# Three placements in on-chip memory moved by 16, 32 and 64 bytes

## The reference

```python
for l in range(2):
    hc, hx = ada_ffn_half(hc, ...), ada_ffn_half(hx, ...)      # first SwiGLU
    uc, ux = modulate(rms_norm(hc)), modulate(rms_norm(hx))
    yc, yx = token_mixing(uc, ux, ...)                         # three branches
    hx = hx + gate * yx
    hx = ada_ffn_half(hx, ...)                                 # second SwiGLU
    if l == 0: hc = hc + gate * yc; hc = ada_ffn_half(hc, ...)

ada_ffn_half = h + 0.5 * gate * ((silu(g) * u) @ w_down),  g, u = split(mod(rms_norm(h)) @ w_gu)
token_mixing: p = u @ w_in;  gMLP branch | bidirectional gated DeltaNet | latent attention;
              y = (sum_b sigmoid(gate_b) * (branch_b @ w_b)) @ w_out
```

## The kernel before

| tensor | start before | start after | step from one part to the next, before | after |
|---|---|---|---|---|
| w_hi | 25728 | 25728 | 4096 a half | 4128 |
| w_lo | 38016 | 38112 | 4096 a half | 4128 |
| h | 50304 | 50560 | 2048 a chunk | 2048 |
| u_hi | 66688 | 66944 | 2048 a chunk | 2064 |
| u_lo | 83072 | 83456 | 2048 a chunk | 2064 |
| arena | 127808 | 128384 | 2048 a slot | 2048 |

## Time and profile before

### The profile page before, as it was taken

The page is one execution under the profiler, slowest core; times in us unless marked ns, Lnnn a source line. Parts: engine busy times, 40 slices in busy tenths (PEclk is TensorE's granted clock), DMA queues, the critical chain, the costliest instruction groups (busy, mean ns, idle before and its releaser), DMA issues.

```text
span 2531.9 us, 37811 instructions
## 1 busy us (share of the span) xinstructions
PE 2430.3 (96%) x15806; PEld 2061.2 (81%) x15806; DVE 1466.0 (58%) x2287; ACT 945.7 (37%) x1537; POOL 90.4 (4%) x122
## 2 busy tenths in 40 slices
PE   5999999999989999999999999999999989999999
PEld 4888877867878888888888788888886878898999
DVE  5877656355667465577655453333354667567555
ACT  2322223365554422232222232322245554444543
POOL 0000000000023000000000000000000003100000
PEclk9999999999999999999999999999999999999999
DMA  7544543201200143335454332222321220055454
GB/s 274 215 181 185 183 150 114 87 34 51 84 35 2 34 166 124 126 117 200 183 199 166 150 110 100 100 96 98 107 100 67 84 84 2 19 177 173 167 184 167
DMA packets 44663, 309.65 MB, mean 122 GB/s; under 512 B 5072, under 2 KB 6224, under 8 KB 7632
## 3 DMA queue, kind: packets, MB, share of 16 engines
q1 hardware_dynamic: 44208, 305.98, 33.5%
q10 hardware_dynamic: 288, 1.27, 0.1%
HBM read 306.18 MB, written 1.05 MB: 121 GB/s over the span
## 4 chain that ended last, share of the span: by engine, by line
PE 89%; DVE 5%; ACT 3%; issue 2%; DMA 1%; SPq 0%; POOL 0%; ACTq 0%; DVEq 0%
PE bank L1475 74%; PE bank L1841 7%; PE bank L1468 2%; PE bank L1778 1%; PE bank L1757 1%; DVE w_lo L2097 1%; DVE u_lo L2144 1%; DVE sq L2136 1%; PE bank L1506 1%; ACT w_hi L933 1%; PE bank L1691 1%; DMA mod_par<-in_mod 0%; PE bank L1518 0%; PE bank L1766 0%; ACT work L1246 0%
## 5 line engine op out<-in xcount | busy, mean ns | idle before, releaser
L2097 DVE TENSOR_TENSOR w_lo<-ring,w_hi 128x1024 fp32r<-128x1024 f32 x420 | 510.5, 1224 | 676.5 <-ACT w_hi L933 671.7
L1475 PE MATMUL bank<-u_hi,w_hi 128*128 128x512 f32 (+1 forms) x2272 | 816.7, 359 | 27.9 <-DVE w_lo L2097 14.9
L1475 PE MATMUL bank<-u_hi,w_lo 128*128 128x512 f32 (+1 forms) x2272 | 805.8, 355 | 0.0
L1475 PE MATMUL bank<-u_lo,w_hi 128*128 128x512 f32 (+1 forms) x2272 | 805.3, 354 | 0.0
L933 ACT ACTIVATE w_hi<-ring 128x1024 fp32r<-128x1024 f32 x420 | 442.9, 1059 | 837.7 <-PE bank L1475 824.1
L1475 PEld LDWEIGHTS bank<-u_hi,w_hi 128*128 128x128 f32 x2272 | 432.9, 191 | 95.6 <-issue 21.6
L1475 PEld LDWEIGHTS bank<-u_lo,w_hi 128*128 128x128 f32 x2272 | 433.0, 191 | 59.4
L1475 PEld LDWEIGHTS bank<-u_hi,w_lo 128*128 128x128 f32 x2272 | 433.3, 191 | 56.8
L1475 PE MATMUL bank<-hidden_hi,w_hi 128*128 128x512 f32 (+1 forms) x722 | 260.6, 361 | 0.0
L1475 PE MATMUL bank<-hidden_lo,w_hi 128*128 128x512 f32 (+1 forms) x722 | 259.9, 360 | 0.0
L1475 PE MATMUL bank<-hidden_hi,w_lo 128*128 128x512 f32 (+1 forms) x722 | 259.9, 360 | 0.0
(11 more groups left out here) (236 smaller groups left out, 2458.1 us busy)
## 6 DMA issues: line engine op xcount, KB each, us to landing
ring<-in_wts SPq DMA_DIRECT2D x288, 1024.0 KB, 4.8
h<-in_x SPq DMA_DIRECT2D x8, 256.0 KB, 4.1
par<-in_par ACTq DMA_DIRECT2D x2, 620.0 KB, 6.0
out<-h SPq DMA_DIRECT2D x8, 128.0 KB, 4.2
cst<-in_cst SPq DMA_DIRECT2D x1, 704.0 KB, 11.8
mod_par<-in_mod SPq DMA_DIRECT2D x1, 96.0 KB, 12.0
cond<-in_c SPq DMA_DIRECT2D x1, 8.0 KB, 1.8
```

The costliest lines, as they stand in the source:

```text
L1475: last = weights.used(pe.matmul(out, lhs[a], rhs[b], start=start and n == 0, stop=stop and n == 2))
L2097: tt(w_lo[:, b % HALVES, :], half_source(n % RING, part), w_hi[:, b % HALVES, :].bitcast(F32), ALU.subtract).then_inc(panel_left[n % RING] ...
```

## The change

Nothing is computed differently and no instruction is added, removed or moved: on all five queues the built program has the same instructions in the same order with the same waits. Only addresses change. Each half of w_hi and w_lo gets 8 unused elements (32 bytes) behind it, each chunk of u_hi and u_lo 4 unused elements (16 bytes). 64 unused bytes stand behind the weights and 64 ahead of the arena. The table above has the addresses that come of it.

```diff
+W_GAP = 8
+U_GAP = 4
...
-        w_hi = sb("w_hi", [P, HALVES, HALF], F32R)
-        w_lo = sb("w_lo", [P, HALVES, HALF], F32R)
-
-        products_kept = [nc.alloc_sbuf_tensor_at(f"products_kept{n}", [P, 2 * HALVES, T], F32,
-                                                 offset=weights_at + n * HALVES * HALF * 4) for n in range(2)]
+        w_hi = sb("w_hi", [P, HALVES, HALF + W_GAP], F32R)
+        w_lo = sb("w_lo", [P, HALVES, HALF + W_GAP], F32R)
+
+        products_kept = [nc.alloc_sbuf_tensor_at(f"products_kept{n}", [P, HALVES, HALF + W_GAP], F32,
+                                                 offset=weights_at + n * HALVES * (HALF + W_GAP) * 4) for n in range(2)]
+        sb("behind_weights", [P, 16])
         h = sb("h", [P, DC, T])
-        u_hi = sb("u_hi", [P, DC, T], F32R)
-        u_lo = sb("u_lo", [P, DC, T], F32R)
+        u_hi = sb("u_hi", [P, DC, T + U_GAP], F32R)
+        u_lo = sb("u_lo", [P, DC, T + U_GAP], F32R)
...
         SLOT = T * 4
+        sb("ahead_of_arena", [P, 16])
         base = -(-nc.sbuf_base // 32) * 32
...
-            return [x[:, 2 * b:2 * b + 2, :] for x in products_kept]
+            return [x[:, b, 0:HALF].rearrange("p (d t) -> p d t", t=T) for x in products_kept]
...
-                act.activation(w_hi[:, b % HALVES, :], half_source(n % RING, part), ACT.Copy).then_inc(weights_rounded, 1)
+                act.activation(w_hi[:, b % HALVES, 0:HALF], half_source(n % RING, part), ACT.Copy).then_inc(weights_rounded, 1)
...
-                    return [x[:, b % HALVES, :].rearrange("p (k n) -> p k n", n=width) for x in (w_hi, w_lo)]
+                    return [x[:, b % HALVES, 0:HALF].rearrange("p (k n) -> p k n", n=width) for x in (w_hi, w_lo)]
...
-                tt(w_lo[:, b % HALVES, :], half_source(n % RING, part),
-                   w_hi[:, b % HALVES, :].bitcast(F32), ALU.subtract).then_inc(
+                tt(w_lo[:, b % HALVES, 0:HALF], half_source(n % RING, part),
+                   w_hi[:, b % HALVES, 0:HALF].bitcast(F32), ALU.subtract).then_inc(
```

## The result

The changed kernel takes 2552.93 us (2548.54 at a mean granted clock of 0.988 and 2557.31 at 0.982) against 2534.88 us: a ratio of 1.0069, with a 95% interval from 1.0047 to 1.0092. It is 18 us slower. That lies within the 2% that I called no change and inside my range, but the forecast was 47 us the other way.

The account below looks back on a forecast made before the run. The prediction took the pace of TensorE's fp32r products as the bound. Its terms, -17.4 and -29.9 us for u and 0 for the rest, sum to -47.3 us: 2488 us forecast, range 2435 to 2555.

Parts of the forecast that it names:

- What bounds the kernel: Claimed the pace of TensorE's fp32r products sets the time, 74% of the last-ending chain, with the producers ahead.
- Term 1: Gaps between u's chunks and weight halves: u one step faster, -17.4 us at 256 columns and -29.9 at 512.
- the two steps of the sum: The forecast's -17.4 us for u at 256 columns and -29.9 us for u at 512.
- its own sign of failure: Forecast fails if the sum's first two steps differ in sign, or VectorE's waits before the products grow over 10 us.
- Term 2: Arena 64 bytes later: 0 taken, with 21 us up or 47.5 us down as its range.
- Terms 3 and 4: VectorE and ScalarE at new addresses, and producers or weight transfers becoming late: 0 taken, no gain taken back.
- No net effect: Rival on TensorE's paces: distances are not the cause or their spread only averages, +4 us; 2505 to 2550 us, chance 0.28.
- the case that had a chance of 0.12: The slower outcome, a time above 2550 us.
- Most of the excess goes: Rival: both new spreads avoid a coincidence, saving 68.4 to 142 us on TensorE; 2393 to 2470 us, chance 0.24.
- Slower, by a 64-byte unit: Rival: operand starts off 64 bytes cost one step more, +35.5 us, 2570 us, or 2601 with weights; chance 0.12.
- The page's rule: TensorE's two SBUF reads use independent ports and never wait, so the sum would be 0: 2535 us.

Follow-up runs that it names:

- e1_map: Separate kernel without the backbone: TensorE alone runs groups of 24 fp32r matmuls at many operand distances; 226.6 to 234.6 ns at 512 columns, 113.3 to 120.0 at 256.
- e9_map3: Separate kernel, TensorE's groups of 24 matmuls at 16 distances, six each, after pauses of different length; distance 0 always came to 226.7 ns at 512 columns.
- e2_swap: Kernel before with u and arena exchanging their places modulo 512, weights unmoved, no gaps; 2550.55 us, ratio 1.0063.
- e7_arena: Kernel before with only the 64 bytes ahead of the arena; 2529.88 us against 2534.21, ratio 0.9979.
- e6_starts: Kernel before with w_lo, u and arena starting where the changed kernel has them modulo 512, but no gaps between chunks or halves; 2559.31 us, ratio 1.0099.
- e3_chunks: Kernel before with only the 16 bytes behind each chunk of u, other starts kept modulo 512; 2552.91 us, ratio 1.0071.
- e5_map2: Separate kernel without the backbone, varying weight width, starts by 4 bytes, chunk step and columns; 512-column groups with full-width weights settled between 226.7 and 240.0 ns.
- e11_late: Kernel before with the arena 64 bytes later, and u and hidden of layer 1's last SwiGLU 192 bytes into their chunks; 2526.28 us against 2535.07, ratio 0.9959.
- e8_best: Kernel before with starts moved so that every distance is -16 modulo 256; 2548.55 us, ratio 1.0056.
- e10_halves256: Kernel before with 256-byte gaps between weight halves and the arena 64 bytes later, every distance 0 modulo 256; 2524.81 us, ratio 0.9958.

## Why the prediction was wrong, step by step

- **What bounds the kernel.** Right. TensorE waited no longer for w_lo and u_lo, and the paces alone sum to +19.8 us, where the medians show 18.
- **Term 1, the gaps.** Here the forecast failed: "None is 0 ... At 512 columns ... I take one step less here too, -29.9 us, since the coincidence at the start is gone ..." The row at hand said that distance 0 had the better pace at 512 columns, 226.6 against 233.3 ns. I took the equal starts for a collision and wrote down a gain against that row. e1_map and e9_map3 show 0 modulo 256 as the best place and e2_swap shows its loss in the kernel. The term measured +23.3 us, within the bounds that I gave (-59.7 to +29.9) and near the end that I had passed over. At 256 columns the sign was right and the size too large: -2.6 ns, not a step of 6.7, -6.8 us where I had -17.4, because the gaps spread u over many distances and only a few, such as 112 and 192, give 113.3. So the two steps of the sum were not of one sign, which the prediction had named as its own sign of failure.
- **What led to that step.** Two premises were wrong. The distances were taken modulo 512, while the pattern repeats every 256 bytes (e1_map), so that "None is 0" did not hold either: 256, which is in both spreads of u_hi, is the same place as 0. And one distance was taken to have one pace, although in the kernel before the arena's 256-column products held 113.4 ns with hidden and 116 to 118 with m.
- **Term 2, the arena.** 0 forecast, +3.3 us measured (-2.4 + 5.7). The small sum hides two moves. The 64 bytes alone bring 512 columns to 226.7 ns, -5 us net (e7_arena); with the halves moved too, distance 0 is left and 232.1 ns remain, and 113.4 becomes 118.3.
- **Terms 3 and 4, the other engines.** Right, at 0. VectorE's subtraction takes 1224 ns and ScalarE's rounding 1059 ns, before and after; the row of the first in the page of the changed kernel (count, busy us, mean ns, idle before):

```profile
L2101 DVE TENSOR_TENSOR w_lo<-ring,w_hi 128x1024 fp32r<-128x1024 f32 x420 | 510.6, 1224 | 690.2 <-ACT w_hi L937 685.7
```

- **The rivals.** *No net effect* came nearest to the mechanism: "the spread of distances only averages" foresaw an excess of 16.7 ns at 512 columns and 10.0 at 256; it is 18.5 to 18.8 and 10.7 to 11.6. Some 2 ns more on the 6474 matmuls of 512 columns (+12 us) and about 1 ns more on the 3780 of 256 (+4) are what lies between its +4 us and +20. The measured time lies 3 us above its 2550, in the case that had a chance of 0.12. And it is not the spread that does it: e6_starts, with one distance for each pair of tensors, costs the same. *Most of the excess goes* is false: nothing under 226.6 and 113.3 ns in any placement. *Slower, by a 64-byte unit* had the sign and not the mechanism (e3_chunks).
- **The page's rule.** By the Trainium skill's page "SBUF — State Buffer", section "Who interferes with whom", the two reads of TensorE go through independent ports, and the time would not have moved. The measurement decides against that: with no other engine at work the same matmul has a pace of 226.6 to 240.0 ns by its placement and its entry (e1_map, e5_map2, e9_map3). Whether one of the two reads waits for the other, no run shows.

## What to carry to other kernels

Where matmuls of this kind bound a kernel, divide pieces of the chain by their counts for each tensor and width, and compare them with the addresses modulo 256 before moving anything: a placement that already has the better of two paces is evidence for itself, whatever seems to collide there. Keep halves, chunks and slots multiples of 256 bytes apart, so that one distance holds throughout, and set it by width (0 for 512 columns, as measured here; for 256 columns 192, which e11_late used, or 112, which drew every entry of e9_map3 to 113.3 ns but was tried in no kernel). Measure a placement with pauses in front of it, since one group after another can show a pace that the kernel will not keep.

## What the runs showed of the hardware that was not expected

- One fp32r product, 128x128 by 128x512, holds paces from 226.7 ns (the best) over 231 to 232 and 233.3 to 236.7 and 240.0 at a granted clock of 1.00; 128x256 has 113.3 at best and 120.0 at worst for distances that are multiples of 16 bytes. The distance between its two operands modulo 256 bytes decides which of them are open to it, and the entry which is taken.
- Over one column a cycle, 13.3 ns remain at best from 320 to 512 columns (146.7, 173.3, 200.0, 226.7 ns). At 128 and 192 columns the pace is 111.6 ns for both, so the columns do not set it there; that the weight load does is likely but not shown, since its width was not varied at those columns.
- A stretch can run for 160 us at 226.7 ns and another of the same placement at 233.3 for 55 us (e8_best), which a timing of the whole kernel shows only as their sum.

Open: what in TensorE makes the fixed 13.3 ns and the steps above it. Theory X, by which it was the width of the weights, is excluded; no run here looks inside. Open too is why a lower granted clock costs e2_swap and e11_late more than the kernel before, and why e10_halves256, whose paces promise 5.4 us, gave 10.3.
